# Hybrid encoder on Trainium2: an expert's ranks dealt over the partitions, and the next pair's gate matmuls between turning and down

## The reference

```
g_idx = argmax(xt @ w_rg + b_rg)                       # 1 group of 4
top_v, top_i = top_k(e_logits of that group, 2)        # 2 experts of its 8
combine = one_hot(g_idx) * softmax(top_v) * p(group)
h = silu(xt @ w_gate[e]) * (xt @ w_up[e])              # 1024 -> 256, for each of 32 experts e
out += (h * combine[e]) @ w_down[e]                    # 256 -> 1024
```

## Time and profile before

| | us |
|---|---|
| median of 3 runs | 669.41 |
| lowest, highest | 668.88, 674.28 |
| profiled execution | 672.68 |
| its span | 670.9 |
| PE busy in the span | 586.4 (87%) |
| DVE busy | 267.8 (40%) |
| ACT busy | 209.9 (31%) |
| POOL busy | 93.9 (14%) |
| DMA, mean rate over the span | 227 GB/s |

### The profile page before, as it was taken

The page is one execution under the profiler, slowest core; times in us unless marked ns, Lnnn a source line. Parts: engine busy times, 40 slices in busy tenths (PEclk is TensorE's granted clock), DMA queues, the critical chain, the costliest instruction groups (busy, mean ns, idle before and its releaser), DMA issues. The chain is left out here.

```text
span 670.9 us, 8837 instructions
## 1 busy us (share of the span) xinstructions
PE 586.4 (87%) x3390; PEld 437.8 (65%) x3391; DVE 267.8 (40%) x578; ACT 209.9 (31%) x404; POOL 93.9 (14%) x125
## 2 busy tenths in 40 slices
PE   3999998998999989999999947999999977777881
PEld 3789878777588868888888845555554544444550
DVE  4555747435423566433362674121111111112356
ACT  3454446445393722422331321011011000000123
POOL 3000404000001101100000123211211211100034
PEclk9999999999988999999999975999999999999996
DMA  7474111102312221268786292899999999999963
GB/s 233 112 253 150 54 50 39 27 0 64 94 32 64 63 63 33 64 221 291 301 329 238 101 362 102 321 415 419 419 420 417 420 420 420 419 418 421 416 258 125
DMA packets 57008, 152.04 MB, mean 227 GB/s; under 512 B 8184, under 2 KB 38160, under 8 KB 44304
## 3 DMA queue, kind: packets, MB, share of 16 engines
q1 hardware_dynamic: 51840, 141.53, 55.8%
q0 software_dynamic: 5008, 9.99, 4.0%
q10 hardware_dynamic: 128, 0.09, 0.0%
HBM read 147.37 MB, written 12.60 MB: 238 GB/s over the span
## 5 line engine op out<-in xcount | busy, mean ns | idle before, releaser
L1037 PE MATMUL bank<-slots,xgT 128*64 128x256 f32 x640 | 74.2, 389 | 10.3 <-DMA slots<-expert_w_up 5.0
L1037 PEld LDWEIGHTS bank<-slots,xgT 128*64 128x64 f32 x640 | 47.6, 140 | 39.9 <-issue 12.9
L1614 DVE TENSOR_TENSOR w_low<-w,w_high 128x1024 fp32r<-128x1024 f32 x32 | 39.2, 1225 | 84.7 <-ACT w_high L1278 84.7
L692 PE MATMUL bank<-x_high,w_high 128*128 128x512 f32 x168 | 67.9, 404 | 1.0 <-DVE x_low L1543 1.0
L692 PE MATMUL bank<-x_high,w_low 128*128 128x512 f32 x168 | 66.5, 396 | 0.0
L692 PE MATMUL bank<-x_low,w_high 128*128 128x512 f32 x168 | 66.5, 396 | 0.0
L1278 ACT ACTIVATE w_high<-w 128x1024 fp32r<-128x1024 f32 x32 | 33.8, 1056 | 53.5 <-PE bank L692 53.5
L1901 DVE TENSOR_TENSOR h_sb<-h_silu,bank 128x256 f32<-128x256 f32 x14 | 5.9, 421 | 110.2 <-ACT h_silu L1421 110.2
L1057 PE MATMUL bank<-slots,hT 128*64 128x512 f32 x160 | 36.5, 598 | 10.8 <-DVE hT L1905 7.0
L692 PE MATMUL bank<-w_high,x_high 128*128 128x420 f32 x128 | 45.3, 354 | 0.4 <-DVE w_low L1534 0.4
L1421 ACT ACTIVATE h_silu<-bank 128x256 f32<-128x256 f32 x14 | 5.4, 383 | 127.6 <-PE bank L1037 127.6
(11 more groups left out here) (266 smaller groups left out, 1117.3 us busy)
## 6 DMA issues: line engine op xcount, KB each, us to landing
slots<-expert_w_gate SPq DMA_DIRECT2D x22, 1024.0 KB, 23.0
slots<-expert_w_up SPq DMA_DIRECT2D x22, 1024.0 KB
slots<-expert_w_down SPq DMA_DIRECT2D x22, 1024.0 KB, 23.2
slot2a<-expert_w_gate SPq DMA_DIRECT2D x10, 1024.0 KB
slot2b<-expert_w_up SPq DMA_DIRECT2D x10, 1024.0 KB, 25.4
w<-w_in SPq DMA_DIRECT2D x16, 512.0 KB, 3.9
w<-w_in SPq DMA_DIRECT2D x8, 840.0 KB, 4.6
slot2b<-expert_w_down SPq DMA_DIRECT2D x5, 1024.0 KB
```

Of the source, the lines that this page charges most:

```text
L692: ins_ = mm(out_, stat[a_], mov[b_], start=first and q_ == 0, stop=last and q_ == 2)
L1037: ins = mm(bank[2][e * SLOTS:(e + 1) * SLOTS, m * FE:(m + 1) * FE], xgT[:, c, e * SLOTS:(e + 1) * SLOTS], gu[m][e][:, c], start=(c == 0), ...
L1614: V.tensor_tensor(wl2[:, u % 2, :], raw2[:, u % 2, :], wh2[:, u % 2, :].bitcast(F32), ALU.subtract).then_inc(s["lo_done"], 1)
```

## The change

It has two parts that don't need each other.

**Places.** The slot number is now xored with the number of the pair, and the one-hot matrix is written in another order: partition 32x + 4e + l holds slot 32x + 8l + e (e of 0 to 7, l of 0 to 3). So eight successive ranks of an expert lie four partitions apart, and the first rank begins in another place in each pair. For that a fifth row of `pi` is used and the integer operations stand in another order (9 instructions in place of 8, with 4 in place of 5 ordered waits). The comparison reads `iota` through a view with a step of 8. All tables come from the same `hot`, so gather, scatter and the slot weights agree.

**Order on TensorE.** `gate_up` is split into gate (m = 0) and up (m = 1). The gate waits for ScalarE's half of `xgT` ahead of its first product and for VectorE's half only ahead of its fifth c. Gate of pair n+1 is issued between `turn_h(n)` and `down(n)`; the first pair's gate stands ahead of the loop. Pairs 14 and 15 are unchanged.

```diff
-            def gate_up(n, slot, loads):
+            def gate_or_up(n, m, slot, loads):
                 gu, _ = slot_views(slot)
-                pe.wait_ge(s["xgt_outA"], n + 1)
-                pe.wait_ge(s["xgt_outD"], n + 1)
-                for m in range(2):
-                    pe.wait_ge(m_in[slot][m], 32 * loads)
-                    for c in range(KC):
-                        for e in range(2):
...
+                pe.wait_ge(m_in[slot][m], 32 * loads)
+                for c in range(KC):
+                    if m == 0 and c == 0:
+                        pe.wait_ge(s["xgt_outA"], n + 1)
+                    if m == 0 and c == KC // 2:
+                        pe.wait_ge(s["xgt_outD"], n + 1)
+                    for e in range(2):
...
             def pair(n, k, round_, following=True):
-                gate_up(n, k, round_ + 1)
+                gate_or_up(n, 1, k, round_ + 1)
                 if following:
-                    turn_x(n + 1, (k + 1) % 3, round_ + 1 + (k + 1) // 3)
+                    k1, loads1 = (k + 1) % 3, round_ + 1 + (k + 1) // 3
+                    turn_x(n + 1, k1, loads1)
                 turn_h(n)
+                if following:
+                    gate_or_up(n + 1, 0, k1, loads1)
                 down(n, k, round_ + 1)
             turn_x(0, 0, 1)
+            gate_or_up(0, 0, 0, 1)
...
-            link(V.tensor_scalar(pi[:, 3, :], pi[:, 0, :], 2, (ROUNDS - 1) * PAIRS, ALU.logical_shift_right, ALU.bitwise_and))
-            link(V.tensor_tensor(pi[:, 1, :], pi[:, 1, :], pi[:, 2, :], ALU.bitwise_or))
-            link(V.tensor_scalar(pi[:, 2, :], pi[:, 0, :], 10, None, ALU.logical_shift_right))
-            link(V.tensor_tensor(pi[:, 3, :], pi[:, 3, :], pi[:, 2, :], ALU.bitwise_or))
+            V.tensor_scalar(pi[:, 3, :], pi[:, 0, :], 2, (ROUNDS - 1) * PAIRS, ALU.logical_shift_right, ALU.bitwise_and)
+            link(V.tensor_scalar(pi[:, 4, :], pi[:, 0, :], 10, None, ALU.logical_shift_right))
+            V.tensor_tensor(pi[:, 1, :], pi[:, 1, :], pi[:, 2, :], ALU.bitwise_or)
+            link(V.tensor_tensor(pi[:, 3, :], pi[:, 3, :], pi[:, 4, :], ALU.bitwise_or))
+            link(V.tensor_tensor(pi[:, 1, :], pi[:, 1, :], pi[:, 4, :], ALU.bitwise_xor))
...
+            dealt = K["iota"].rearrange("p (x l e) -> p x e l", l=4, e=8)
             for k in range(2 * NT):
-                V.tensor_scalar(hot[:, k, 0, :], K["iota"], pf[:, 0, k:k + 1], None, ALU.is_equal)
+                V.tensor_scalar(hot[:, k, 0, :].rearrange("p (x e l) -> p x e l", l=4, e=8), dealt, pf[:, 0, k:k + 1], None, ALU.is_equal)
```

More of the change, by code:

```diff
@@ L145, in hybrid_encoder @@
         place = sb("place", [P, 2 * NT])
-        pi = sb("pi", [P, 4, 2 * NT], I32)
+        pi = sb("pi", [P, 5, 2 * NT], I32)
         pf = sb("pf", [P, 2, 2 * NT])
@@ L1027, in turn_x @@
                         ins.then_inc(s["xt_done"], 1)
-            def gate_up(n, slot, loads):
+            def gate_or_up(n, m, slot, loads):
                 gu, _ = slot_views(slot)
-                pe.wait_ge(s["xgt_outA"], n + 1)
-                pe.wait_ge(s["xgt_outD"], n + 1)
-                for m in range(2):
-                    pe.wait_ge(m_in[slot][m], 32 * loads)
-                    for c in range(KC):
-                        for e in range(2):
-                            ins = mm(bank[2][e * SLOTS:(e + 1) * SLOTS, m * FE:(m + 1) * FE], xgT[:, c, e * SLOTS:(e + 1) * SLOTS],
-                                     gu[m][e][:, c], start=(c == 0), stop=(c == KC - 1), skip_group_check=True)
-                    ins.then_inc(s[("g_done", "u2_done")[m]], 1)
+                pe.wait_ge(m_in[slot][m], 32 * loads)
[5 more added lines that the diff above has]
+                    for e in range(2):
+                        ins = mm(bank[2][e * SLOTS:(e + 1) * SLOTS, m * FE:(m + 1) * FE], xgT[:, c, e * SLOTS:(e + 1) * SLOTS],
+                                 gu[m][e][:, c], start=(c == 0), stop=(c == KC - 1), skip_group_check=True)
+                ins.then_inc(s[("g_done", "u2_done")[m]], 1)
             def turn_h(n):
@@ L1089, in _ @@
                             turn_x(n, 1, dv + 6)
-                            gate_up(n, 1, dv + 6)
+                            gate_or_up(n, 0, 1, dv + 6)
+                            gate_or_up(n, 1, 1, dv + 6)
                             turn_h(n)
```

## The result

The changed kernel took 661.39 us (median of 4 runs, 659.6 to 664.03) beside 669.14 us of the kernel before (668.7 to 674.28): a ratio of 0.986, 95% interval 0.983 to 0.990, so 7.75 us less. Two later comparisons gave 0.988 (0.984 to 0.992) and 0.989 (0.986 to 0.993). Of the cases written down, rival B (663.0) came nearest.

The account below looks back on a forecast made before the run. DMA, streaming expert weights with no free time from 424 to 640 us, was taken as the bound. Terms -4.2 + 0.2 - 0.7 + 1.8 + 1.2 - 0.4 = -2.1 us gave 667.3 us, range 662.5 to 672.5.

Parts of the forecast that it names:

- rival B: Spread of rows pays in full and TensorE's order costs nothing that matters: -6.4, so 663.0 us; chance 0.14.
- Part 1: Ranks' places, DMA-bound expert stage: evener rows per engine land gate 13's weights earlier, -4.2 us (bounds 0 and 5.6).
- The reckoning by the rows of the heaviest engine: End of weight stream: 37 rows at 0.17 us each, so the last DMA would end 6.3 us earlier.
- Part 2: VectorE's table work: eight comparisons reading iota with a stride cost +0.2 us (bounds 0 to 0.6).
- Part 3: First gate at stage start: waits only for ScalarE's half of xgT, starts earlier, -0.7 us (up to 2.4).
- Part 4: Stage start: gate ahead of down delays the first down load, a one-time DMA gap of +1.8 us (bounds 0.5 to 2.5).
- Part 5: Late loop: gate 13 ahead of down 12 puts up 13 7.0 us behind gate 13, +1.2 us (bounds 0.8 and 2.1).
- Part 6: Kernel's end: GpSimd's additions start earlier and hold VectorE's row additions up less, -0.4 us (bounds 0 and -1.5).
- A: TensorE's clock falls in the new long wait before a gate, +2.7 at pair 13, so 670.0 us; chance 0.27.
- C: Ranks don't spread, or the DMA lag isn't theirs; the 4.2 us go, so 671.5 us; chance 0.10.
- D: Clock falls before gate 13 and stays at 1.2 GHz through the tail: +12, so 679 us; chance 0.07.

Follow-up runs that it names:

- Crowding: Kernel before with eight successive ranks on four neighbouring partitions and the four 32 above, one DMA engine's: 683.45 us, ratio 1.018.
- the two kernels without gathers: All gather indices out of bounds, so gathers move no rows: on the kernel before 658.91 us, on the new places with TensorE's old order 653.28 us.
- the two waits alone: Kernel before with only the gate's single place of waiting for both xgT halves split in two, order and places as before: 668.5 us, ratio 0.997.
- mending that one place: Changed kernel with gate 13 put back behind down 12, the new order kept in the earlier pairs: 663.49 us, ratio 0.991.

## Why the prediction came out as it did

**Part 1, the places: the step that failed.** It said that "the most that an even spread can give at the end is the 6.0 us", hence bounds of 0 and 5.6 at gate 13, and took 4.2. Measured with the places alone, gate 13 starts 5.9 us earlier against the first gate load (5.6 to 5.9 in the four profiles with even places and the old order), at or above the upper bound. The mechanism was right, and the lag alone was well sized (3.6 of 4.2). What the step left out is the rate. It took a share of 1.02 to mean that there was nothing to gain in the saturated stretch, and looked for the loss in the decline alone. Yet the share counts engines that are busy, not what they move: 419 GB/s became 425 at a lower share, which is the 2.3 us that go beyond the lag.

The reckoning by the rows of the heaviest engine that was weighed there gave 6.3 us, nearer to what came than the sum's own value; but it holds only in part. Crowding put 67 more rows on the heaviest engine for 12.4 us, 0.19 us a row; the even places took 37 off for 7.8, 0.21 a row; yet the two kernels without gathers, 75 and 58 rows, differ by 4.1 us in the last two pieces of their profiles and 6.7 by their medians on two chips, 0.24 to 0.39 a row. Over 2 us of each of the last two differences are the rate, which doesn't go by the number of rows. So no fixed price of a row comes out of these runs.

**Part 2, small VectorE work.** The eight strided comparisons take 0.33 us each, where one took 0.29, and the series of products that waits for them 4.00 us instead of 3.64 (before, then changed):

```profile
403.49 3.64 PE L1013 MATMUL bank<-hot 128*128 128x128 f32 x8 [3.62 <-DVE hot L1872]
```

```profile
398.48 4.00 PE L1013 MATMUL bank<-hot 128*128 128x128 f32 x8 [3.60 <-DVE hot L1880]
```

+0.36 for the +0.2 forecast, inside its bounds.

**Part 3, the first gate: right in mechanism, too small.** The gate starts 0.9 us earlier behind the tables, as worked out. But the clock rose earlier too, the case for which the part named up to 2.4 us and of which it took 0.7: with two waits it rises 1.1 to 3.7 us behind the gate's start, with one wait 3.7 to 6.0. In the changed kernel's profile it is 2.3, and the first gate load comes 5.0 us behind the gate's start, against 6.2 before. The whole is worth 2.3 us by the first piece of the profiles, and the two waits alone gained 2.2 by the medians.

**Part 4, the gap at the start: too large.** SP's down load comes 2.6 us later, as worked out (2.7). The gap in the flow that was to follow, 1.8 us, is 0.3: only one window is low.

```profile
428.00:429.00 1.00, 1.00 (x12) 0.70 (x10) 0.00 (x0) 0.00 (x0) 0.64 (x1) 1.00 0.72 246
429.00:430.00 1.00, 1.00 (x12) 0.43 (x6) 0.00 (x0) 0.00 (x0) 0.58 (x2) 1.00 1.03 426
```

The count of what was queued had the 4 MiB of weights and left out the rows of two gathers, 0.52 MB in 415 to 429, that are 1.2 us of flow.

**Part 5, the order at the end.** The spacing was exact, 6.94 us for 7.0. Its price was 1.2 us (bounds 0.8 and 2.1): from gate 13 to the end, the changed kernel needs 70.5 us at full clock where the places alone need 68.7, so 1.8; within the bounds. But mending that one place brought nothing by the medians, so that this is the price of that place alone isn't shown.

**Part 6, the end.** Forecast 0.4 less, bounds 0 and 1.5. Places alone: 68.7 against 70.3, so 1.6 less, just beyond the bound. In the sum the measured pieces are -5.9 + 0.4 - 2.3 + 0.3 + 1.8 - 1.6 = -7.3 us, against -2.1 forecast and -6.3 to -7.75 measured. The rate of part 1, which the sum put at nothing, is the largest of the differences (2.3), then the first gate (1.6), the gap of part 4 (1.5) and the end (1.2). Four terms missed to the same side; that rival B's number came near is in part luck, since it has neither the rate nor the first gate's worth.

**The rivals.** A, the clock: the mechanism is there. The granted clock is 0.95 in 440 to 600, gates behind waits of 4.4 to 4.9 us take 5.4 to 6.3 us, and the Trainium skill's rule (TensorE: Matmul & The Clock Gate, HAM oscillation) agrees in that. It reached gate 13 in two of the changed kernel's three profiles and cost 1.1 us more from there on (71.6 against 70.5), not 2.7. Against the rule as stated, it doesn't happen at every wait: a pair at the low clock takes longer, the next wait is then 0.4 to 2.4 us, and behind most of these the clock holds. In the five profiles with the moved gate, all 15 waits of 4.2 to 6.5 us ended in a gate that took 5.0 to 6.5 us; of the waits of 2.2 to 2.4 us some did (5.36) and some didn't (3.67). The old order isn't free of it: in the two waits alone, for one, down 12 takes 5.35 us instead of 3.65, but the granted clock in 440 to 600 stays at 0.99. B, the spread in full: nearest by its number, right that the gap hardly comes and that the end gains 1.5 (1.6 measured), wrong in taking 5.6 as the whole of the spread and 0.7 as that of the first gate. C fell with the crowded ranks. D didn't come: behind the cold gate 13 the next matmuls took 3.60 and 3.62 us.

## What to carry to other kernels

A DMA share of 1.0 says that the engines are busy, not that they move all they can: compare the GB/s of a saturated stretch between kernels. Where sparse indirect rows run beside a large stream, count the rows by the engine that their partition belongs to, and deal successive rows out over all engines. Size such a gain from two places, the decline at the end and the rate in the middle. Where TensorE restarts at the low clock and a stream waits for it, a wait taken out of the restart was worth more than its own length here, 2.3 us for 0.9, since the clock also rose earlier. A reorder in this DMA-bound loop that gathers several short waits into one long one saved nothing and dropped TensorE's clock.

## What the runs showed of the hardware that was not expected

The rate of a saturated stretch depended on where the sparse rows lie: 425 GB/s with successive rows dealt out one by one (with or without the xor) and 419 with four in a row on one engine, at shares of 1.01 and 1.02; and 424 against 418 with half of the rows. It is the weight packets themselves that take longer, 314 ns for 8 KiB instead of 309. With eight in a row the rate was 420 up to 500 us and 398 in 500 to 600, with a few packets of up to 1.9 us.

Whether the longer packets come from several rows of one transfer standing behind each other on an engine, or from the unevenness summed over a transfer, or from engines that are out of step, these runs don't separate: dealing changes all of them, and no kernel was run that has the one without the others.
